# The modulation vector of a transformer block: weights turned so that the input channel lies on the partitions, with a matmul reduction per group

## The reference

```python
def second_block(x, c, w_ada, b_ada, ...):
    mod = jax.nn.silu(c) @ w_ada[l] + b_ada[l]          # [1, 2048] @ [2048, 12288]
    shift_m, scale_m, gate_m, shift_f, scale_f, gate_f = jnp.split(mod[:, None, :], 6, axis=-1)
    h = rms_norm(x, norm_mix_g[l]) * (1.0 + scale_m) + shift_m
    ...
    x = x + gate_m * mix
    h = rms_norm(x, norm_ffn_g[l]) * (1.0 + scale_f) + shift_f
    x = x + gate_f * conv_ffn(h, ...)
```

## Time and profile before

| | us |
|---|---|
| median of 3 runs | 2646.98 (2645.09 to 2654.66) |
| profiled execution, its own time | 2654.66 |
| its span, first to last instruction | 2652.8 |
| TensorE busy | 2567.6 |
| VectorE busy | 2037.3 |
| ScalarE busy | 1327.9 |

### The profile page before, as it was taken

The page is one execution under the profiler, slowest core; times in us unless marked ns, Lnnn a source line. Parts: engine busy times, 40 slices in busy tenths (PEclk is TensorE's granted clock), DMA queues, the critical chain, the costliest instruction groups (busy, mean ns, idle before and its releaser), DMA issues.

```text
span 2652.8 us, 47930 instructions
## 1 busy us (share of the span) xinstructions
PE 2567.6 (97%) x14464; PEld 2223.9 (84%) x14464; DVE 2037.3 (77%) x3154; ACT 1327.9 (50%) x2049; POOL 5.2 (0%) x13
## 2 busy tenths in 40 slices
PE   7999999999999999999997999979899999999997
PEld 6888888888888888888886888858688888888886
DVE  7678675588887887887888547676788888888888
ACT  5334434465554454544554346544545545546456
POOL 0000000000000000000000000000000000000000
PEclk9899999999999999999998999999899999999999
DMA  8686683557788888888885454415455655656554
GB/s 292 225 273 215 214 276 130 171 186 249 270 283 279 281 285 278 280 284 277 283 279 171 162 174 153 146 48 189 136 184 170 201 186 169 202 174 190 188 167 155
DMA packets 160539, 561.89 MB, mean 212 GB/s; under 512 B 17987, under 2 KB 18284, under 8 KB 160492
## 3 DMA queue, kind: packets, MB, share of 16 engines
q1 hardware_dynamic: 132284, 459.04, 52.4%
q10 hardware_dynamic: 27792, 101.20, 11.7%
q0 software_dynamic: 416, 1.06, 0.2%
HBM read 559.12 MB, written 2.11 MB: 212 GB/s over the span
## 4 chain that ended last, share of the span: by engine, by line
PE 93%; DVE 4%; ACT 1%; issue 1%; DMA 0%; DVEq 0%; ACTq 0%; SPq 0%
PE bank L282 93%; DVE w_lo L900 1%; DVE scratch L1216 1%; DVE R L933 0%; DMA X<-in_x 0%; DVE ss L963 0%; ACT w_hi L535 0%; PE bank L383 0%; ACT H L564 0%; DMA ada_w<-in_w_ada 0%; PE bank L374 0%; DVE ss L1320 0%; DVE Z L1468 0%; DVE G L1357 0%; DVE scratch L933 0%
## 5 line engine op out<-in xcount | busy, mean ns | idle before, releaser
L282 PE MATMUL bank<-H,w_hi 128*128 128x512 f32 x4672 | 1665.6, 400 | 33.0 <-DVE H L1222 17.3
L282 PE MATMUL bank<-H,w_lo 128*128 128x256 f32 x4672 | 1317.3, 282 | 0.0
L900 DVE TENSOR_TENSOR w_lo<-w_raw,w_hi 128x1024 fp32r<-128x1024 f32 x900 | 1091.9, 1222 | 142.6 <-ACT w_hi L535 134.6
L282 PEld LDWEIGHTS bank<-H,w_hi 128*128 128x128 f32 x4672 | 884.2, 189 | 251.6 <-issue 26.6
L535 ACT ACTIVATE w_hi<-w_raw 128x1024 fp32r<-128x1024 f32 x900 | 910.4, 1051 | 0.1
L282 PEld LDWEIGHTS bank<-H,w_lo 128*128 128x128 f32 x4672 | 890.2, 191 | 0.1
L282 PE MATMUL bank<-U,w_hi 128*128 128x512 f32 x1984 | 699.9, 396 | 5.4 <-DVE U L1449 4.8
L282 PE MATMUL bank<-U,w_lo 128*128 128x256 f32 x1984 | 557.9, 281 | 0.0
L550 ACT ACTIVATE scratch<-bank 128x256 f32<-128x256 f32 x356 | 136.6, 384 | 835.5 <-PE bank L282 828.3
L282 PEld LDWEIGHTS bank<-U,w_hi 128*128 128x128 f32 x1984 | 372.4, 188 | 97.4 <-DVE U L1449 6.1
L282 PEld LDWEIGHTS bank<-U,w_lo 128*128 128x128 f32 x1984 | 373.8, 188 | 0.0
(11 more groups left out here) (197 smaller groups left out, 1190.4 us busy)
## 6 DMA issues: line engine op xcount, KB each, us to landing
w_raw<-in_w_ff SPq DMA_DIRECT2D x256, 512.0 KB, 5.1
ada_w<-in_w_ada ACTq DMA_DIRECT2D x192, 512.0 KB, 4.5
w_raw<-in_w_up SPq DMA_DIRECT2D x176, 512.0 KB, 4.2
w_raw<-in_w_z SPq DMA_DIRECT2D x96, 512.0 KB, 4.5
w_raw<-in_w_in SPq DMA_DIRECT2D x88, 512.0 KB, 3.9
w_raw<-in_w_gate SPq DMA_DIRECT2D x64, 512.0 KB, 4.6
w_raw<-in_w_down SPq DMA_DIRECT2D x64, 384.0 KB, 3.0
w_raw<-in_w_down SPq DMA_DIRECT2D x64, 320.0 KB, 3.3
```

The lines of the kernel that those rows point to most:

```text
L282: return nc.tensor.matmul(out, lhsT, rhs, start=start, stop=stop, skip_group_check=True)
L900: TT(w_lo[:, slot, :], w_raw[:, slot, :], w_hi[:, slot, :].bitcast(F32), ALU.subtract)\
```

## The change

A block of `w_ada` now holds 128 input channels on the partitions and 1024 output columns along the free dimension. 16 such blocks in a row make one *group* of 1024 columns; there are 12 groups. silu(c) is a column per block, `silu_c` (128x16), made of a new field `c` of the vectors with one small sigmoid and one small product. VectorE adds each block, times its scalar, to `ada_acc` (128x1024). Once 16 blocks are in, the sum over the partitions is left: TensorE makes it with eight matmuls with a weight block of `ada_acc` and a column of ones (`ada_reduce`), and VectorE then clears `ada_acc` and adds `b_ada` into `mod` (`take_mod`). The DMAs of the rows go, and so do `ada_sum` and its two sums. The ff groups of ScalarE and VectorE are now a loop over the first three and a fourth written out.

```diff
-        ada_w = sb("ada_w", [P, 2, ADA_K])
-        c_rows = [Z[:, 40:44, :].rearrange("p a t -> p (a t)"), Z[:, 32:36, :].rearrange("p a t -> p (a t)")]
+        ada_w = sb("ada_w", [P, 2, ADA_COLS])
+        ada_acc = Z[:, 40:44, :].rearrange("p a t -> p (a t)")
...
-            load_c_row(sp, 0)
...
+            def ada_reduce(group):
+
+                pe.wait_ge(sem("ada_acc"), 1 + 16 * group + 16)
+
+                pe.wait_ge(sem("mod_ready"), group)
+                for b in range(ADA_COLS // P):
+                    last = mm(bank[5][:, b:b + 1], ada_acc[:, b * P:(b + 1) * P], ones[:, 0:1], b == 0, True)
+                last.then_inc(sem("ada_reduced"), 1)
...
             with pe.Fori(0, 8) as i:
                 pair_of_units(PAIR0["conv_in"] + i, H, NC)
+            ada_reduce(1)
...
             def ff2(g):
+                ada_reduce(2 * g + 4)
                 with pe.Fori(0, 8) as i:
                     pair_of_units(PAIR0["ff"] + 16 * g + 8 + i, U, NC, "ff.u_ready", 16 * g)
+                ada_reduce(2 * g + 5)
...
-            c_sigmoid(0)
+            A(small[:, 16:32], V("c", 0, 16), ACT.Sigmoid).then_inc(sem("c_sig"), 1)
...
-            load_c_row(act, 1)
...
-            c_sigmoid(1)
...
-            for g in range(FF_GROUPS):
-                ff_group(g, g == FF_GROUPS - 1)
+            with act.Fori(0, FF_GROUPS - 1) as g:
+                ff_group(g, False)
+            ff_group(FF_GROUPS - 1, True)
...
-            def add_ada(chunk, row, par):
+            def add_ada(chunk, k, par):
 
                 dve.wait_ge(sem("ada_landed%d" % par), turn_value(chunk, par))
-                STT(ada_w[:, par, :], ada_w[:, par, :], 1.0, c_rows[row], ALU.mult, ALU.mult,
-                    accum_out=ada_sum[:, bass.ds(chunk, 1)]).then_inc(sem("ada_acc"), 1)
-
-            def silu_row(n):
-
-                dve.wait_ge(sem("c_sig"), n + 1)
-                link(TT(c_rows[n], c_rows[n], c_sigs[n], ALU.mult))
+                dve.wait_ge(sem("ada_acc"), chunk + 1)
+                STT(ada_acc[:, :], ada_w[:, par, :], silu_c[:, bass.ds(k, 1)], ada_acc[:, :], ALU.mult, ALU.add)\
+                    .then_inc(sem("ada_acc"), 1)
...
+            def take_mod(group):
+
+                dve.wait_ge(sem("ada_reduced"), group + 1)
+                v.memset(ada_acc[:, :], 0.0).then_inc(sem("ada_zeroed"), 1)
+                dve.wait_ge(sem("ada_zeroed"), group + 2)
+                n = ADA_COLS // P
+                TT(mod[:, bass.ds(group * n, n)], bank[5][:, 0:n], V("b_ada", group * n, n), ALU.add)\
+                    .then_inc(sem("mod_ready"), 1)
...
-            silu_row(0)
+            dve.wait_ge(sem("ada_zeroed"), 1)
+            dve.wait_ge(sem("c_sig"), 1)
+            link(TT(silu_c[:, :], V("c", 0, 16), small[:, 16:32], ALU.mult))
...
-            dve.wait_ge(sem("ada_acc"), 1 + 2 * ADA_BLOCKS)
-            link(TT(mod[:, :], ada_sum[:, 0:ADA_BLOCKS], ada_sum[:, ADA_BLOCKS:2 * ADA_BLOCKS], ALU.add))
-            link(TT(mod[:, :], mod[:, :], V("b_ada", 0, ADA_BLOCKS), ALU.add))
+            dve.wait_ge(sem("mod_ready"), ADA_GROUPS)
...
-        "w_ada": a["w_ada_2"][0].reshape(2, ADA_K, ADA_BLOCKS, P).transpose(0, 2, 3, 1).reshape(-1, P, ADA_K),
-        "c_row": a["c_2"],
+        "w_ada": a["w_ada_2"][0].reshape(NC, P, ADA_GROUPS, ADA_COLS).transpose(2, 0, 1, 3).reshape(-1, P, ADA_COLS),
```

More of the change, by code:

```diff
@@ L43 @@
 PIECE = FIRST_CHUNKS * P
-ADA_K = 1024
-ADA_BLOCKS = 6 * D // P
+ADA_COLS = 1024
+ADA_GROUPS = 6 * D // ADA_COLS
 CONV_CH = 12
@@ L537, in load_sigmoid @@
             def load_sigmoid():
-                A(small[:, 16:17], V("g_mix"), ACT.Sigmoid)
+                A(small[:, 16:17], V("c"), ACT.Sigmoid)
             def load_ada(chunk, slot):
@@ L964, in _, with plain_normed @@
                 .then_inc(sem("norm.squares"), 1)
-            def plain_normed(name, pair, par, out, chunk=None, total=total, scale=R[:, :]):
+            def plain_normed(name, pair, par, out, chunk=None, k=None, total=total, scale=R[:, :]):
                 if chunk is not None:
-                    add_ada(chunk, 0, par)
+                    add_ada(chunk, k, par)
                 n = add_halves(pair, par, total[par])
@@ L997, in _ @@
                     plain_normed("gate", PAIR0["gate"] + i, par, flat(G[:, bass.ds(i, 1), par, :]),
-                                 ADA0["gate"] + 2 * i + par)
+                                 ADA0["gate"] + 2 * i + par, 2 * i + par)
+            take_mod(0)
             dve.wait_ge(sem("soft.half"), 2)
@@ L1014, in _ @@
                     m = 2 * i + par
-                    plain_normed("conv_in", PAIR0["conv_in"] + i, par, zb(m), ADA0["conv_in"] + m,
+                    plain_normed("conv_in", PAIR0["conv_in"] + i, par, zb(m), ADA0["conv_in"] + m, m,
                                  scale=R_squared if par else R[:, :])
+            take_mod(1)
             with dve.Fori(0, 4) as i:
@@ L1145, in _ @@
                     pair, m = PAIR0["mix"] + i, 2 * i + par
-                    add_ada(ADA0["mix"] + m, 0, par)
+                    add_ada(ADA0["mix"] + m, m, par)
                     n = add_halves(pair, par, total[par])
@@ L1157, in _ @@
             signal_squares("n2", "mix")
+            take_mod(3)
             inverse("n2")
@@ L1174, in ff_group @@
                         split_low(pair + i + 1, par, 1)
+                take_mod(2 * g + 4)
                 if final:
@@ L1193, in ff_group @@
                             TT(ssg, ssg, conv[par], ALU.add).then_inc(sem("ff.ssg"), 1)
-            for g in range(FF_GROUPS):
-                ff_group(g, g == FF_GROUPS - 1)
+                take_mod(2 * g + 5)
+            with dve.Fori(0, FF_GROUPS - 1) as g:
+                ff_group(g, False)
+            ff_group(FF_GROUPS - 1, True)
             signal_squares("n3", "ff")
@@ L1543, in layout @@
         "conv_w": np.concatenate([columns(a["conv_w"][0, j]) for j in range(3)], 1),
-        "b_f": row(a["b_f"]), "g_final": columns(a["g_final"]),
+        "b_f": row(a["b_f"]), "g_final": columns(a["g_final"]), "c": columns(a["c_2"]),
         "b_ada": columns(a["b_ada_2"]), "g_mix2": columns(a["norm_mix_g_2"]), "g_attn": columns(a["attn_norm_g_2"]),
```

24 lines of the change are left out of this document (10 added, 14 removed).

## The result

| | before | after |
|---|---|---|
| median of the runs | 2650.34 us (4 runs, 2645.09 to 2654.66) | 2675.4 us (4 runs, 2673.95 to 2677.19) |
| ratio, 95% interval | 1 | 1.0096 [1.0082, 1.011] |
| span of the profiled execution | 2652.8 us | 2671.0 us |

The changed kernel is slower by 25.1 us, where 25 were forecast; on the median of three runs from which the forecast started, 2672 us were foretold. The two profiled spans lie only 18.2 us apart.

The account below looks back on a forecast made before the run. TensorE, busy 97% of the span, was taken as the bound. Reductions and waits 23.4, start −1.0 and clock falls +3.0 make 25.4 us; 2646.98 + 25 = 2672 us, with unknown pieces giving 2664 to 2682; stated range 2660 to 2690.

Parts of the forecast that it names:

- The reduction's own time: TensorE at group ends: 16 records of 0.111 us, so 1.8 us per reduction at the high clock.
- early ends: After conv_in and the first three ff2: VectorE's last product is over in time, no bubble; 4 x 1.8 = 7.2 us.
- The late ends: Ends of mix and four ff1: TensorE waits for VectorE's last product, 0.35 us each on top of 1.8; 10.8 us.
- qk and n3: Before the attention and norm n3: reductions hide in TensorE's idle time, but take_mod delays VectorE; +1.2 us each.
- take_mod, loops, products at no cost: take_mod at the other ten ends, ff loops on ScalarE and VectorE, and VectorE's products: 0 us each.
- Rival 4: VectorE falls behind, splits come late after each reduction: up to 1.2 us at ten places, 2684 us; chance 0.06.
- The clock: TensorE's clock falls behind two of nine dense reductions, 1.6 us each: +3 us, bounds 0 and nine falls.
- Rival 1: TensorE's clock falls at nearly every reduction: about +39 us, 2686 us; chance 0.12.
- The start and gate: Start: shorter wait chain cuts TensorE's 1.46 us stall, −1.0 us. Gate's end: reduction partly at low clock, +3.0 us.
- rival 2: TensorE's matmul stream takes its tighter rhythm in slow stages behind reductions: +12 us, 2659 us; chance 0.11.
- Rival 3: Every f32 matmul costs four weight loads instead of two, at ten places: +18 us, 2690 us; chance 0.06.

Follow-up runs that it names:

- thin matmuls alone: Kernel before plus eight one-column f32 matmuls on a block of ones at the twelve reduction places, without waits; 2668.12 us, ratio 1.0074.
- the loops alone: Kernel before with only the ff-group loops: first three groups on ScalarE, second and third on VectorE; 2645.57 us, ratio 0.9987.
- The second call: The changed kernel run once more, unaltered, against the kernel before on the same chip; 2675.67 us, ratio 1.0115.
- former late ends: Changed kernel with odd products of mix and the four ff1 cut to 128 columns, two traces; 2665.95 us, ratio 1.0077, and 2666.21 us.

## Why the prediction was right

- **The reduction's own time** (9 x 1.8): right in kind, 6% too large. It is 1.70 us, since two starts mostly lie 0.106 us apart (1.59 us over 15 intervals) and not 0.111. At a few early ends, that of conv_in in each trace of the changed kernel, it is 0.110 or 0.111 and the step 1.76; behind a wait it is 0.113. The kernel with the thin matmuls alone shows this term by itself: 9 x 1.70 = 15.3 us in its steps, 20 in its timing, which has the one at gate too.
- **The late ends** (+0.35 each): a late end costs 0.28 us more than an early one, 0.37 at mix. The wait's place and cause were read rightly from the earlier trace rows, its size was not: at the four ff1 it is 0.15 to 0.17 us (0.27 to 0.29 instead of 0.12), half of the 0.35. The rest is the slower pitch behind it, which the sum had in no term, so the near fit is luck in part.
- **qk and n3** (1.2 each): 1.54 and 1.23. Moving take_mod takes away all of the first and a third of the second, and leaving out the last memset as well takes the rest, and the run without reductions keeps both: VectorE's queue, as stated. What the prediction didn't see is that at n3 the same work would be in the way once more behind the signal.
- **take_mod, loops, products at no cost**: right at the nine dense ends, with steps of 0.01 us or less once TensorE's part is out, and wrong by 0.4 us in the second unit of the first ff1. There the register work that VectorE has to do before its first product made a split late. That is within the bounds given for the loops (0 to 1 us). Rival 4 is out but for this one place.
- **The clock** (two falls, 3.0): two in each trace of the changed kernel, 3.3 us in the first. The number two was picked between bounds of 0 and nine, and four traces have 1 to 3, so that it fits is luck. At the length of 1.7 to 1.8 us a fall came only where a wait stood ahead; the prediction had only said that the late ends are nearer to a fall. The length counts as well: at twice of it all four ends without a wait had a fall. Rival 1 is out at this length, and nearly true at twice of it. The price of one fall by the prediction's formula is 1.54 us and not 1.6; measured are 1.5 to 1.7.
- **The start and gate** (−1.0 and +3.0): this step failed. The stall was 0.26 us in the first trace, below the 0.45 forecast, but TensorE goes on later, at 44.53 instead of 43.72 us. The stall was no sign of the change either: it is 0.29 us in the second trace of before, and from none to 1.90 us in the seven traces with the full reductions. The third block of `w_ada` in the chain of waits at the start, before and now:

```profile
35.94 4.90 DMA ada_w<-in_w_ada
```

```profile
33.92 0.10 DVE silu_c L991
...
34.04 1.30 DVE Z L922
35.36 6.12 DMA ada_w<-in_w_ada
```

  The product of the row did shrink to 0.1 us and the DMA started 0.6 us earlier, but in this trace it took 6.12 us where it had taken 4.90. In seven traces with the full reductions TensorE is 0.3 to 1.9 us later at this point than in the first trace of before, and in its second trace it is 0.5 later as well, so the 1.0 us did not turn up anywhere. At the end of gate the low clock takes in more or less of conv_in. Up to the first matmul of conv_mul, less the reduction at conv_in, the seven traces cost −0.7 to +2.6 us, 0.95 in the mean, for the 2.0 forecast. The start of before itself moves by as much: its second trace is 0.7 us shorter up to there, that of the loops alone 1.6. So the size of this term stays open.
- **Rhythm**, rival 2, which was held to be the other side of the bet: it happened in both directions. The third ff1 in the changed kernel, w_hi alone, in 70 us as in the earlier trace rows:

```profile
1080.00:1150.00 70.00, 70.00 (x199) 37.23 (x199) 29.41 (x24) 25.18 (x24) 1.00 0.78 273
```

  The same stage had the tight rhythm before. The three tight ff1 were lost (+5.3 us), while branch, conv_mul, three up stages and others became tight. In the first trace all this together gave 4.4 us back; in the second, with the up stages slack, it gave hardly anything, and its delay at the end is 24.6 us.

With the means of the traces the sum is 19.6 (eleven steps) + 1.0 (start and gate) + about 3.3 (two falls) + 0.4 (first ff1) = 24 us, against 25.1 in the timing and 20 for TensorE's loads alone. The forecast of 25.4 is 1.1 us too high at start and gate and 0.8 at the steps, and 0.3 too low at the falls and 0.4 at the loops. The second call gave 30 us, so agreement within a microsecond with the first is luck; what the steps show is the kind and size of each term. Rival 3 is out by the count of records. No version tried beats the kernel before: even the one without any reduction was not faster.

## What to carry to other kernels

On an engine that is busy 97% of the time, count the starts of the records that a new step puts into its queue. The busy time that it takes off or puts on another engine counts only where the first engine waits for it: here 22 us more on VectorE cost 2.8 us at two places before a wait of TensorE (qk, n3), some 1.5 at the late ends and nothing at the other ends, and 1.7 us on TensorE cost 1.7 us each time. A restructured loop can cost at its entry: here VectorE's register work and wait before the first product of the ff groups cost TensorE 0.4 us, in the one place right behind a norm. A wait of 0.2 us ahead of a thin stretch can cost more by what the clock does after it than by itself, so the last product before such a stretch should be made early; no run here did so without leaving work out. When a step is moved out of the way of a signal, look at what is queued behind it for the answer to that signal.

## What the runs showed of the hardware that was not expected

- A stage of 16 units takes 88.4 or 90.1 us with the same instructions, 22 units 121.7 or 124.0, and hardly anything between. Such a rhythm holds for a whole stage. In the two traces of before it was the same in all stages from conv_mul to the last ff2, and different behind; in the changed kernel five earlier stages differ as well. Of the 4.4 us between the two traces of before, the up and down stages make 3.6. Of the 6.4 between the two of the changed kernel they make 8.1, the five earlier stages take about as much back (7.4), and the rest comes from the end of gate (2.8) and the stages from in2 to out2 (2.7). A change that touches nothing in a stage can still turn its rhythm. What draws the rhythm stays open.
- Eight matmuls with f32 weights and one column cost 1.69 to 1.76 us when they follow dense work at once, and 1.81 us behind a wait. One matmul of 8 columns costs 0.24 to 0.35 us.
- Fall of the clock behind a thin stretch of 1.7 us: none at 28 early ends without a wait in seven traces, at 10 former late ends and at the nine places of the thin matmuls alone; 11 at 25 ends with 0.15 us or more of wait ahead of it. With twice the matmuls seven of nine, among them all four without a wait. A fall of 3.4 us cost 1.5 to 1.7 us, one of 6.8 us made its stage 2.8 us longer.
